# Four early projections load both dense slots of a round ahead of the round's two modulation slots

## What is computed

```python
shift, scale, gate = jnp.split(c_act @ mod_w[layer] + mod_b[layer], 3, axis=-1)
h = modulate(rmsnorm(x, norm_g[layer]), shift, scale)
u, z = jnp.split(h @ w_in, 2, axis=-1)        # projections u and z, then a state space scan over u
...
y = y * jax.nn.sigmoid(y @ w_glu + b_glu)     # projection glu
return (y * jax.nn.silu(z)) @ w_out           # projection out
...
kv = (h_kv @ w_kv)                            # projection kv, after a norm that the new x and its modulation feed
proj = h @ w_qg                               # q is its first 2048 columns
```

## Time and profile before

| | |
|---|---|
| median of 3 runs | 3174.06 us |
| profiled execution, its own time | 3175.62 us |
| its span (first to last instruction) | 3173.9 us |
| PE busy | 3096.3 us, 98% |
| DVE busy | 1783.8 us, 56% |
| ACT, POOL busy | 499.7 us, 275.3 us |
| HBM read | 591.6 MB, 187 GB/s over the span |
| mean granted TensorE clock | 0.995 |

### The profile page before, as it was taken

One profiled execution on the slowest core, in us unless ns is written; L12 is line 12 of the kernel. 1 busy time (PEld: TensorE's weight loads), 2 busy tenths in 40 slices (PEclk: granted clock), 3 DMA queues, 4 the chain that ended last, 5 costly groups with the idle time before them and its releaser, 6 DMA issues.

```text
span 3173.9 us, 54906 instructions
## 1 busy us (share of the span) xinstructions
PE 3096.3 (98%) x23204; PEld 2843.5 (90%) x23204; DVE 1783.8 (56%) x2769; ACT 499.7 (16%) x1012; POOL 275.3 (9%) x143
## 2 busy tenths in 40 slices
PE   6899999999999999999999999999999999999999
PEld 4788888888889888898888888899999999999999
DVE  5349964453354455564637844667665555555443
ACT  2206510100000334211300012220000000000000
POOL 2002210000001555220000000000100000000000
PEclk9999999999999999999999999999999999999999
DMA  9874568766664323243353432424444444444443
GB/s 406 324 298 187 199 260 338 317 242 262 259 246 160 133 107 133 107 166 134 133 189 141 155 120 107 155 96 171 186 160 172 172 159 173 171 159 173 170 161 132
DMA packets 51168, 597.36 MB, mean 188 GB/s; under 512 B 9551, under 2 KB 12334, under 8 KB 13998
## 3 DMA queue, kind: packets, MB, share of 16 engines
q1 hardware_dynamic: 50990, 594.79, 48.5%
HBM read 591.60 MB, written 3.16 MB: 187 GB/s over the span
## 4 chain that ended last, share of the span: by engine, by line
PE 89%; DVE 4%; DMA 3%; issue 1%; DVEq 1%; ACT 1%; POOLq 0%; POOL 0%; SPq 0%; ACTq 0%
PE bank L2827 25%; PE bank L845 21%; PE bank L301 14%; PE bank L794 11%; PE bank L333 3%; DMA ring<-in_t_mod 3%; PE bank L347 2%; PE bank L791 2%; DVE E L378 1%; PE bank L618 1%; PE aux L1822 1%; PE bank L424 1%; PE bank L608 1%; PE aux L1869 1%; PE bank L1058 0%
## 5 line engine op out<-in xcount | busy, mean ns | idle before, releaser
L845 PE MATMUL bank<-hT,ring 128*128 128x128 f32 x3776 | 458.3, 276 | 1.0 <-POOLq L1807 1.0
L845 PEld LDWEIGHTS bank<-hT,ring 128*128 128x128 f32 x3776 | 439.0, 192 | 15.0 <-issue 13.3
L2827 PE MATMUL bank<-arena,ring 128*128 128x128 f32 x3440 | 396.4, 275 | 0.0
L2827 PEld LDWEIGHTS bank<-arena,ring 128*128 128x128 f32 x3440 | 390.2, 192 | 0.0
L794 PE MATMUL bank<-hT,ring 128*128 128x256 f32 x1472 | 321.8, 380 | 0.0
L301 PE MATMUL bank<-arena,ring 128*128 128x256 f32 x1472 | 321.3, 380 | 0.5 <-ACT arena L1356 0.5
L301 PEld LDWEIGHTS bank<-arena,ring 128*128 128x128 f32 x1472 | 278.6, 190 | 39.9 <-issue 2.0
L794 PEld LDWEIGHTS bank<-hT,ring 128*128 128x128 f32 x1472 | 278.4, 190 | 39.6 <-issue 2.5
L301 PE MATMUL bank<-hT,ring 128*128 128x256 f32 x960 | 211.4, 382 | 4.7 <-issue 4.7
L301 PEld LDWEIGHTS bank<-hT,ring 128*128 128x128 f32 x960 | 183.3, 192 | 31.5 <-issue 6.5
L845 PE MATMUL bank<-arena,ring 128*128 128x128 f32 x1728 | 207.9, 275 | 1.5 <-DVEq L658 1.5
(11 more groups left out here) (461 smaller groups left out, 3982.3 us busy)
## 6 DMA issues: line engine op xcount, KB each, us to landing
ring<-in_t_mod SPq DMA_DIRECT2D x64, 2048.0 KB, 13.3
ring<-in_t_gu SPq DMA_DIRECT2D x44, 2048.0 KB, 7.9
ring<-in_t_out SPq DMA_DIRECT2D x16, 2048.0 KB, 8.0
ring<-in_t_zs SPq DMA_DIRECT2D x16, 2048.0 KB, 7.9
ring<-in_t_down SPq DMA_DIRECT2D x16, 2048.0 KB, 7.4
ring<-in_t_gdn SPq DMA_DIRECT2D x12, 2048.0 KB, 7.8
ring<-in_t_u SPq DMA_DIRECT2D x8, 2048.0 KB, 9.0
ring<-in_t_z SPq DMA_DIRECT2D x8, 2048.0 KB, 7.8
```

The costliest lines, as they stand in the source:

```text
L845: last = nc.tensor.matmul(out[:, P * at:P * at + P], a[:, j, :], tile_at(b, j), start=j == 0 and q in (0, 3), stop=j == half - 1 and q in ...
L2827: last = nc.tensor.matmul(out[:, P * q:P * q + P], a[:, j, :], b[:, j, :], start=begins and q == 0 and j == 0, stop=ends and q == len(grou ...
```

## The change

One condition and one branch in `stream_mixed`:

```diff
-                        if k % 2 == (0 if name != "kv" or (i, p) == (0, 0) else 1):
+                        if k % 2 == (0 if name == "z" or (i, p) == (0, 0) else 1):
                             rows(p)
 
-            if name in ("u", "kv"):
+            if name != "z":
                 for i in range(COUNT[name] // 8):
                     turn(i)
             else:
```

## The result

| | before | changed |
|---|---|---|
| median | 3174.19 us (4 runs, 3172.79 to 3179.39) | 3213.34 us (4 runs, 3207.29 to 3216.4) |
| ratio to before | | 1.0118, 95% interval 1.0107 to 1.013 |
| span of the profiled execution | 3173.9 us | 3214.6 us |
| mean granted clock | 0.995 | 0.991 |

The change makes the kernel 39 us slower. I had forecast 21, with 28 as the upper end. The direction was right, the size was not.

The account below looks back on a forecast made before the run. PE, busy 98% of the span, was taken as the bound. Ends 13.7, out's late B 3.3, kv's start 2.5 and clock 1.7 sum to 21.2 us, added to the 3174.06 us median: 3195.3 us, range 3186 to 3202.

Parts of the forecast that it names:

- What bounds the kernel: Whole kernel: PE is busy 98% of the span, so only taking idle time from PE helps and added idle time hurts.
- Round 3 at the ends: Last sums of u, glu, out and q: PE waits 3.2, 3.7, 3.4 and 3.4 us for DVE's pair, together 13.7 us.
- 17.7 us from the issue of B to the landing of M: All changed projections: M lands 17.7 us after B's issue, as in kv, with the pair done after 30.6 us.
- whether M follows B at once or 2.6 us later: Loads of M: issue 0.4 or 2.6 us after B changes nothing, because B's transfer is in the way in either case.
- B of round 0 behind M: Start of out: M of round 0 goes out late with B behind it, so PE waits 3.3 us for B.
- The start of kv: From out's end into kv: 1.5 us for DVE's updates and scaled copy, 1.1 us or more for kv's B; together 2.5 us.
- Rounds 1 and 2: u, glu, out and q: later sums are wanted only after the next round's A, 14 us later, so cost is hidden.
- The clock: PE after the six added pauses: one drop to the lower clock, 1.7 us, with bounds 0 and 10 us.
- B would come late because it shares the transfer with M: Rival: B lands with all three transfers after 17.7 us, PE waits 4.5 us in 12 rounds; about 3228 us; chance 5%.
- M would land soon enough to hide everything: Rival: M lands within 14.5 us of B's issue, end waits and late Bs vanish; 3175 us; chance 4%.

Follow-up runs that it names:

- round 3 alone: Changed kernel, but order A, B, M only in round 3 of u, glu, out and q, with rounds 1 and 2 back at A, M, B: 3202.11 us, ratio 1.0081.
- ACT's copies ahead: Changed kernel, but in out ACT copies product m+1 ahead of the squares of m: 3201.7 us, ratio to before 1.0084.
- glu alone: Changed kernel with order A, B, M kept in glu only, u, out and q back at A, M, B: 3184.75 us, ratio to before 1.0034.

## Why the prediction was right and wrong

**What bounds the kernel: right.** No dense slot waited for a transfer before, so there was nothing to win, and every wait added at PE stayed to the end.

**Round 3 at the ends: right in kind, a little small.** I had 3.2, 3.7, 3.4 and 3.4 us for u, glu, out and q. The kernel with round 3 alone shows 15.8 us in sum against my 13.7, because M landed later than I had reckoned. In the changed kernel u has 3.20 and q 3.96, but glu 5.60. The term that was too small is that of 17.7 us from the issue of B to the landing of M. In glu M of round 1 goes out right behind B, which is issued at 429.79, and DVE's wait for M ends 18.8 us later:

```profile
448.61 0.49 DVE L376 TENSOR_SCALAR E<-ring,c_act 128x512 f32<-128x512 f32 x1 [18.11 <-DMA ring<-in_t_mod]
```

In u and out it is 18.5 and 18.6 us in the same situation. I had said that it makes no difference whether M follows B at once or 2.6 us later. It makes about 1 us in these three, and why is open; it is not the same everywhere (17.5 us in glu of the kernel with ACT's copies ahead). As each M can go out only when the last pair has freed its slots, the delay stays until the end. That gives glu the 4.3 to 4.5 us of the three other kernels with a wait there; the 5.60 of the changed kernel is a further 1.2 us because M of round 3 took 15.9 us from its issue to the end of DVE's wait instead of 14.7 with glu alone, and this varies between kernels with the same order in glu.

**B of round 0 behind M: right for out, smaller.** Forecast 3.3 us; 2.58 in the changed kernel, 1.1 to 3.5 in four others. The start of kv: 1.34 us of L518 as forecast (1.5), but no wait for kv's B in the changed kernel (I had 1.1), since PE came later and slower.

**Rounds 1 and 2: wrong, and this is the first step that failed.** I wrote "The sums of rounds 1 and 2 are wanted only after A of the next round, 14 us later than in round 3 ... hidden". I asked who waits for the pair's result, and not who waits for what DVE does behind the pair. In out DVE's updates of x stand behind the pair, ACT's squares wait for the updates, ACT's next copy stands behind the squares, and that copy frees a slot of the ring. I had even listed these updates in the kernel's description, and used them only at the end of out. Forecast for out with the start of kv: 3.4 + 2.5 us, and measured alone 19.2. The repair at ACT and the kernel with old rounds 1 and 2 both recover 11 to 13 us, so this cost is shown and sized by two runs. They give back waits and the clock behind them together; the waits alone are 8.1 us in out (5.2 us for dense slots and 2.9 us at its end).

**The clock: wrong in size, the second step that failed.** I took "one, 1.7 us", with 10 us as the upper bound, because kv's wait of 3.1 us had left the clock at 1.00. In the changed kernel's profile the same wait of kv is followed by low clock, as are the ends of u and out (windows of the changed kernel; the columns are those of the earlier trace rows):

```profile
222.00:232.20 10.20, 6.90 (x78) 5.62 (x79) 8.19 (x16) 3.88 (x9) 0.00 (x0) 0.52 0.82 321
648.70:658.90 10.20, 7.12 (x24) 5.41 (x25) 5.21 (x11) 3.06 (x4) 2.53 (x2) 0.52 0.74 284
771.50:778.30 6.80, 6.20 (x22) 4.72 (x23) 0.69 (x2) 0.27 (x1) 0.00 (x0) 0.52 0.77 284
```

0.52 is close to the lower of the two levels, 1.2 GHz against 2.4. At the end of u part of this is not from the wait: the kernel before has 0.86 from 222.0 to 232.2 us. By medians the clock is what is left of 39.2 us when 28.9 of waits are taken off, 10 us; with round 3 only it is 26.7 - 18.9 = 8 us. One profile of the kernel before was too little to price this: that a wait of 3.1 us left the clock alone in one execution does not say that it does so in the next, and six of nine profiles show a fall behind this same wait. The waits of 4.0 to 7.1 us at the other ends were followed by one each time. The Trainium skill ("TensorE: Matmul & The Clock Gate", HAM oscillation) describes a kernel in which PE is throttled again at each wait for data. The runs agree with that for the twelve waits of 4.0 to 7.1 us, and for six of the nine in kv; my upper bound of 10 us, which went by it, came nearer than the one drop that I took.

**Rivals.** That B would come late because it shares the transfer with M (3228 us) did not happen: in u, glu and q no dense slot of rounds 1 to 3 waits, and in the changed kernel B lands 7.7 to 8.1 us after its issue with M right behind it. That M would land soon enough to hide everything did not happen either.

## What to carry to other kernels

When a step on one engine comes later, follow everything that is queued behind it on that engine, and everything that waits for those, until a resource is freed: a late result that nobody needs yet can hold a buffer that the next load needs. Waits at an otherwise full PE can cost more than their length, since slower products may follow: 18.9 us of waits cost 26.7 us with the new order in round 3 only. One profile does not price such a wait. Moving a small wait behind other ready work, as with kv's last sums, can pay: 5.5 us (2 to 8) for a wait of 3.1. And with a bound engine that is 98% busy, an earlier load of its inputs is worth nothing unless the trace shows it waiting for one.

## What the runs showed of the hardware that I had not expected

After pauses of 3 to 7 us PE's products are mostly slower for a while: 64 records of 128x256 in 15.77 us (out, round 3) or 16.67 us instead of 14.08. The second stands behind kv's end in the changed kernel:

```profile
772.68 16.67 PE L347 MATMUL bank<-ring,arena 128*128 128x256 f32 x64
```

The change of clock does not follow every pause, and the same kernel's profile can have it or not: kv's end in the kernel before stayed at 1.00 after 3.13 us of idleness, and fell to 0.52 in the changed one after 3.09. Keeping PE busy in the pauses with products that nobody reads brought its busy time, without them, from 3110.3 back to 3097.5 us.

Three transfers of 2 MB in one queue landed in the order of their issue, also when two follow at once: B after 7.7 us, the first modulation slot after 12.2 us and the second some 18 us after its issue (glu, round 1). The one issued first was not slowed by those behind it: B took 7.7 to 8.0 us with M right behind it in round 1 of the four projections, and 7.8 us in kv's round 3 before, where M followed 2.65 us later.
